# One-core hybrid encoder step: the final normalisation done inside the expert blocks, and three weight homes in place of two

## The reference

```python
def grouped_experts(t, experts, gates, wg, wu, wd):
    ...
    def run(args):
        xb, e = args
        return (jax.nn.silu(xb @ wg[e]) * (xb @ wu[e])) @ wd[e]

    ys = lax.map(run, (xs, blk_exp)).reshape(R, t.shape[1])
    ys = ys * row_gate[:, None].astype(ys.dtype)
    return jax.ops.segment_sum(ys, row_tok, num_segments=N + 1)[:N]
...
        yp = yp + hier_moe(rmsnorm(yp, norm2_w[l]), ...)
...
def rmsnorm(x, w):
    xf = x.astype(F32)
    y = xf * lax.rsqrt(jnp.mean(xf * xf, axis=-1, keepdims=True) + RMS_EPS)
    return (y * w.astype(F32)).astype(x.dtype)
```

## Time and profile before

| | |
|---|---|
| median of 3 runs | 2894.78 us (2892.29 to 2896.38) |
| the profiled execution's own time | 2889.87 us |
| its span, first to last instruction | 2888.1 us |
| PE busy | 2686.8 us, 93% |
| DVE busy | 1494.0 us, 52% |
| ACT busy | 720.3 us, 25% |
| POOL busy | 664.2 us, 23% |
| moved by DMA | 404.42 MB, mean 140 GB/s |
| mean granted PE clock | 0.968 of 2.4 GHz |

### The profile page before, as it was taken

How to read it: one execution, slowest core, us unless ns; L and a number is a source line. 1 busy time by engine, 2 the same in 40 slices (tenths; PEclk the granted TensorE clock), 3 DMA queues, 4 the chain that set the end, 5 groups by cost and what they waited for, 6 DMA issues and landing times. The chain is left out here.

```text
span 2888.1 us, 38265 instructions
## 1 busy us (share of the span) xinstructions
PE 2686.8 (93%) x11801; PEld 1617.9 (56%) x11802; DVE 1494.0 (52%) x2787; ACT 720.3 (25%) x2014; POOL 664.2 (23%) x921
## 2 busy tenths in 40 slices
PE   8999999999999986999999999499999999999990
PEld 6777777777777765555555555244444444444430
DVE  2565655556655564676777775434343434343333
ACT  1222222122222213555556664000000000000004
POOL 2111111111111111112222222223233333333330
PEclk9999999999999997999999999599999999999995
DMA  6010001000010046322121212299888688886877
GB/s 249 31 36 26 25 25 40 29 33 25 25 36 33 26 135 239 117 88 79 53 88 45 66 63 78 77 374 308 299 266 279 198 280 277 288 278 211 268 236 269
DMA packets 225977, 404.42 MB, mean 140 GB/s; under 512 B 30866, under 2 KB 88594, under 8 KB 225888
## 3 DMA queue, kind: packets, MB, share of 16 engines
q1 hardware_dynamic: 172976, 342.30, 33.4%
q0 software_dynamic: 18208, 48.64, 6.7%
q10 hardware_dynamic: 34704, 12.37, 1.7%
HBM read 310.62 MB, written 80.79 MB: 136 GB/s over the span
## 5 line engine op out<-in xcount | busy, mean ns | idle before, releaser
L670 PE MATMUL z_psum<-w_in_sb,hT 128*128 128x512 f32 x1088 | 480.5, 592 | 0.0
L664 PE MATMUL z_psum<-hT,w_in_sb 128*128 128x128 f32 x3264 | 375.2, 276 | 3.0 <-DMA w_in_sb<-in_w_in 3.0
L664 PEld LDWEIGHTS z_psum<-hT,w_in_sb 128*128 128x128 f32 x3264 | 371.0, 193 | 3.8 <-issue 3.8
L1968 PE MATMUL gate_psum<-w_gate_sb,block_rows_T 128*128 x720 | 321.4, 600 | 20.4 <-DMA w_gate_sb<-in_w_e_gate 20.4
L1983 PE MATMUL down_psum<-w_down_sb,hidden_T 128*128 x720 | 318.2, 595 | 7.1 <-DVE hidden_T L1922 7.1
L670 PEld LDWEIGHTS z_psum<-w_in_sb,hT 128*128 128x128 f32 x1088 | 200.5, 190 | 221.0 <-issue 221.0
L1972 PE MATMUL up_psum<-w_up_sb,block_rows_T 128*128 x720 | 316.3, 592 | 0.0
L1636 PE MATMUL y_psum<-w_out_sb,mix_T 128*128 128x512 f32 x512 | 239.7, 612 | 11.2 <-DVE mix_T L1391 11.2
L1265 ACT ACTIVATE w_in_sb<-score_psum,neg_max 128x512 f32<-128x512 f32 (+3 forms) x320 | 196.8, 622 | 209.5 <-DVE neg_max L1352 209.3
L1968 PEld LDWEIGHTS gate_psum<-w_gate_sb,block_rows_T 128*128 128x128 f32 x720 | 138.5, 193 | 195.9 <-issue 195.9
L1983 PEld LDWEIGHTS down_psum<-w_down_sb,hidden_T 128*128 128x128 f32 x720 | 137.4, 191 | 180.8 <-issue 180.8
(11 more groups left out here) (295 smaller groups left out, 3389.7 us busy)
## 6 DMA issues: line engine op xcount, KB each, us to landing
w_gate_sb<-in_w_e_gate SPq DMA_DIRECT2D x32, 2048.0 KB, 13.8
w_up_sb<-in_w_e_up SPq DMA_DIRECT2D x32, 2048.0 KB, 13.3
w_down_sb<-in_w_e_down SPq DMA_DIRECT2D x32, 2048.0 KB, 15.0
w_in_sb<-in_w_in SPq DMA_DIRECT2D x7, 2048.0 KB, 19.1
hidden_by_lane<-hidden ACTq DMA_DIRECT2D x720, 16.0 KB
scratch_z<-z_ring SPq DMA_DIRECT2D x34, 256.0 KB, 2.0
scratch_y<-w_in_sb SPq DMA_DIRECT2D x17, 512.0 KB, 2.6
scratch_h<-h SPq DMA_DIRECT2D x17, 512.0 KB, 2.6
```

The costliest lines, as they stand in the source:

```text
L664: mm = pe.matmul(out[:, hd * P:(hd + 1) * P], w[:, g, c, hd * P:(hd + 1) * P], hT[:, u, c, :], start=(c == 0), stop=(c == DC - 1))
L670: mm = pe.matmul(out[:, :], hT[:, u, c, :], w[:, g, c, :], start=(c == 0), stop=(c == DC - 1))
L1968: mm = pe.matmul(gps[:, :], xT[:, u, c, :], part(wg, slot, c), start=(c == 0), stop=(c == DC - 1))
```

## The change

`finish` is gone. Each expert block now also normalises its rows: Pool gathers the present sums of its 128 tokens (`sums`); DVE adds the gated output to them, both halves (`add`); Pool writes the result back to `y` with a plain scatter; ACT forms the statistics (`stats`); DVE multiplies (`final`) and Pool scatters the product to the output `y_all`, which holds prompt, sample and padding rows in one tensor and is cut apart outside. A token's first block writes a value from an incomplete sum, its second one overwrites it; each final scatter waits for the landing of the one before. The weights have three homes, with the lists (division by 3 in place of 2) to match; the table of the first two runs' `run_before` isn't waited for.

```diff
-            pool.iota(keep["run_slot"][:, :], [[0, P // 2], [-1, 2]], base=1, channel_multiplier=0)
+            pool.iota(keep["run_slot"][:, 0:P - 2], [[0, P // 3], [1, 3]], base=0, channel_multiplier=0)
...
-        wg, wu = sb("w_gate_sb", [P, 2, DC, D_EXP]), sb("w_up_sb", [P, 2, DC, D_EXP])
-        wd = sb("w_down_sb", [P, 2, FC, D])
+        wg, wu = sb("w_gate_sb", [P, 3, DC, D_EXP]), sb("w_up_sb", [P, 3, DC, D_EXP])
+        wd = sb("w_down_sb", [P, 3, FC, D])
...
-                if not isinstance(r, int) or r > 0:
+                if not isinstance(r, int) or r > 1:
                     sp.wait_ge(done, entry("run_before", 1, N_BLOCKS))
...
-            def scatter(b, u):
+            def sums(b, u, finals):
 
                 wait(pool, o_out, 16 * b)
+                wait(pool, f_out[u], 16 * finals)
                 pool.tensor_copy(dest[:, u:u + 1], col(tok_all, b)).then_inc(dest_ok, 1)
                 pool.wait_ge(dest_ok, b + 1)
-                pool.wait_ge(d_act, b + 1)
-                pool.wait_ge(d_dve, b + 1)
+                pool.sem_inc(stand, 1)
+                pool.indirect_dma_start(out=yg[:, u, :], out_offset=None, in_=dr["y"],
+                                        in_offset=bass.IndirectOffsetOnAxis(ap=dest[:, u:u + 1], axis=0)).then_inc(y_in, 16)
+
+            def scatter(b, u):
+                pool.wait_ge(s_ok, b + 1)
                 pool.sem_inc(stand, 1)
                 pool.indirect_dma_start(out=dr["y"], out_offset=bass.IndirectOffsetOnAxis(ap=dest[:, u:u + 1], axis=0),
-                                        in_=out[:, u, :], in_offset=None, compute_op=ALU.add).then_inc(o_out, 16)
+                                        in_=out[:, u, :], in_offset=None).then_inc(o_out, 16)
                 gate_of(b + 2, u)
+
+            def final(b, u, finals):
+                pool.wait_ge(f_ok, b + 2)
+                wait(pool, f_out[1 - u], 16 * finals)
+                pool.sem_inc(stand, 1)
+                pool.indirect_dma_start(out=dr["y_all"], out_offset=bass.IndirectOffsetOnAxis(ap=dest[:, u:u + 1], axis=0),
+                                        in_=fo[:, u, :], in_offset=None).then_inc(f_out[u], 16)
...
             with pool.Fori(1, n) as i:
                 gather(i * 2 + 3, 1)
+                sums(i * 2, 0, i)
+                final(i * 2 - 1, 1, i)
                 scatter(i * 2, 0)
...
-            def copy_out(b, u):
-                act.wait_ge(d_ps, b + 2)
-                wait(act, o_out, 16 * b)
-                act.wait_ge(gate_in[u], 16 * (b // 2) + 16 if isinstance(b, int) else (b - u) * 8 + 16)
-                nc.scalar.activation(out[:, u, 0:HW], dps[:, 0, :], ACT.Copy, scale=gcol[:, u:u + 1]).then_inc(d_act, 1)
+            def stats(b, u):
+
+                act.wait_ge(s_ok, b + 1)
+                wait(act, f_ok, b)
+                chain.after(nc.scalar.activation(junk[:, :], out[:, u, :], ACT.Square, accum_out=st[:, u, 0:1]))
+                chain.after(nc.scalar.activation(st[:, u, 1:2], st[:, u, 0:1], ACT.Ln, scale=1.0 / D, bias=consts["eps"][:, 0:1]))
+                nc.scalar.activation(st[:, u, 2:3], st[:, u, 1:2], ACT.Exp, scale=-0.5).then_inc(r_ok, 1)
 
             def blk(b, u):
                 gate(b)
                 spread_a(b)
-                copy_out(b - 1, 1 - u)
+                stats(b - 1, 1 - u)
...
             with act.Fori(1, n) as i:
+                chain.loop(i - 1, 4)
+                nc.scalar.preload_act_table_set(ACT_SET)
                 blk(i * 2 + 1, 1)
                 blk(i * 2 + 2, 0)
...
-            def copy_out(b, u):
+            def add(b, u):
                 dve.wait_ge(d_ps, b + 2)
-                wait(dve, o_out, 16 * b)
                 dve.wait_ge(gate_in[u], 16 * (b // 2) + 16 if isinstance(b, int) else (b - u) * 8 + 16)
-                ts(out[:, u, HW:D], dps[:, 1, :], gcol[:, u:u + 1], None, ALU.mult).then_inc(d_dve, 1)
-
-            def blk(b, u):
+                dve.wait_ge(y_in, 16 * b + 16)
+                wait(dve, r_ok, b)
+                for half in range(2):
+                    c = slice(half * HW, (half + 1) * HW)
+                    ins = nc.vector.scalar_tensor_tensor(out=out[:, u, c], in0=dps[:, half, :], scalar=gcol[:, u:u + 1], in1=yg[:, u, c],
+                                                         op0=ALU.mult, op1=ALU.add)
+                ins.then_inc(s_ok, 1)
+
+            def final(b, u, finals):
+                dve.wait_ge(r_ok, b + 2)
+                wait(dve, f_out[u], 16 * finals)
+                if isinstance(b, int) and b == 0:
+                    dve.wait_ge(fw_in, 16)
+                nc.vector.scalar_tensor_tensor(out=fo[:, u, :], in0=out[:, u, :], scalar=st[:, u, 2:3], in1=fw[:, :],
+                                               op0=ALU.mult, op1=ALU.mult).then_inc(f_ok, 1)
+
+            def blk(b, u, finals):
                 hidden(b)
                 turn_x(b + 1, 1 - u)
-                copy_out(b - 1, 1 - u)
+                add(b - 1, 1 - u)
                 turn_a(b, u)
-
+                final(b - 1, 1 - u, finals)
...
                 pe.wait_ge(aT_ok, b + 1)
                 pe.wait_ge(d_in, run)
-                wait(pe, d_act, b)
-                wait(pe, d_dve, b)
+                wait(pe, s_ok, b)
...
-def finish(nc, dr, consts):
...
-        finish(nc, dr, consts)
```

More of the change, by code:

```diff
@@ L1566, in _ @@
             chain.after(red(lists[:, 2:3], run_row[:, :], AX.X, ALU.add))
-            chain.after(ts(half[:, :], lists[:, 2:3], 0.5, -0.25, ALU.mult, ALU.add))
-            chain.after(cp(lst[:, 3:4], half[:, :]))
-            stt(out=lists[:, 3:4], in0=lst[:, 3:4], scalar=-2.0, in1=lists[:, 2:3], op0=ALU.mult, op1=ALU.add).then_inc(lst_ok, 1)
+            chain.after(ts(half[:, :], lists[:, 2:3], 1.0 / 3, -2.0 / 3, ALU.mult, ALU.add))
+            chain.after(ts(lst[:, 3:4], half[:, :], -3.0, -1.0, ALU.mult, ALU.add))
+            tt(lists[:, 3:4], lst[:, 3:4], lists[:, 2:3], ALU.add).then_inc(lst_ok, 1)
             dve.wait_ge(blk_in, 16)
@@ L1748, in experts @@
         g_ps, u_ps, eg_ok, a_ok = sem("gate_in_psum"), sem("up_in_psum"), sem("gate_exp_ready"), sem("hidden_ready")
[L1749 to L1751 removed]
+        ar_in, aT_ok, d_ps, s_ok = sem("hidden_spread"), sem("hidden_T_ready"), sem("down_in_psum"), sem("sums_ready")
+        y_in, fw_in, r_ok, f_ok, f_out = sem("sums_gathered"), sem("final_row_loaded"), sem("final_rstd"), sem("final_ready"), [sem(f"final_scattered{u}") for u in range(2)]
+        step_, act_step = sem("p5_dve_step"), sem("p5_act_step")
         stand, sp_stand = sem("p5_pool_stand"), sem("p5_sync_stand")
@@ L1842, in _ @@
             gather(2, 0)
+            sums(0, 0, 0)
             gather(3, 1)
@@ L1845, in _ @@
             gather(4, 0)
+            sums(1, 1, 0)
+            final(0, 0, 0)
             scatter(1, 1)
@@ L1848, in _ @@
                 gather(i * 2 + 3, 1)
+                sums(i * 2, 0, i)
+                final(i * 2 - 1, 1, i)
                 scatter(i * 2, 0)
                 gather(i * 2 + 4, 0)
+                sums(i * 2 + 1, 1, i)
+                final(i * 2, 0, i)
                 scatter(i * 2 + 1, 1)
-            scatter(n * 2, 0)
+            sums(n * 2, 0, n)
+            final(n * 2 - 1, 1, n)
+            final(n * 2, 0, n)
             pool.wait_ge(x_in[0], n * 64 + 128)
             pool.wait_ge(x_in[1], n * 64 + 64)
-            pool.wait_ge(gate_in[0], n * 16 + 32)
+            pool.wait_ge(gate_in[0], n * 16 + 16)
             pool.wait_ge(gate_in[1], n * 16 + 16)
-            pool.wait_ge(o_out, n * 32 + 16)
+            pool.wait_ge(o_out, n * 32)
+            pool.wait_ge(f_out[0], n * 16 + 16)
+            pool.wait_ge(f_out[1], n * 16)
         @block.scalar
@@ L1861, in _ @@
             n = load(act, trips[0:1, 0:1], 1, MAXT)
+            chain = Chain(act, act_step)
             def gate(b):
@@ L1891, in _ @@
             with act.Fori(1, n) as i:
+                chain.loop(i - 1, 4)
+                nc.scalar.preload_act_table_set(ACT_SET)
                 blk(i * 2 + 1, 1)
                 blk(i * 2 + 2, 0)
-            copy_out(n * 2, 0)
+            chain.end_loop(n - 1)
+            nc.scalar.preload_act_table_set(ACT_SET)
+            stats(n * 2, 0)
         @block.vector
@@ L1940, in _ @@
             turn_a(0, 0)
-            blk(1, 1)
-            blk(2, 0)
+            blk(1, 1, 0)
+            blk(2, 0, 0)
             with dve.Fori(1, n) as i:
                 chain.loop(i - 1, 6)
-                blk(i * 2 + 1, 1)
-                blk(i * 2 + 2, 0)
-            copy_out(n * 2, 0)
+                blk(i * 2 + 1, 1, i)
+                blk(i * 2 + 2, 0, i)
+            add(n * 2, 0)
+            final(n * 2, 0, n)
         @block.tensor
@@ L1955, in run_of @@
                 return (load(pe, keep["block_run"][0:1, bass.ds(b, 1)], 16, 16 * N_EXP),
-                        load(pe, keep["block_slot"][0:1, bass.ds(b, 1)], 0, 1))
```

(5 more changed lines are left out.)

66 lines of the change are left out of this document (12 added, 54 removed).

## The result

The changed kernel takes 2918.38 us (2914.58 to 2920.8, 4 runs) against 2895.58 us for the kernel before, ratio 1.0079, interval 1.0061 to 1.0096: slower by 0.8%, 23 us. The profiled execution took 2918.12 us, its span is 2916.3 us, 28.2 more than before. The forecast of 2887.6 had the wrong sign; the time lies in the range, near rival A's 2927.

The account below looks back on a forecast made before the run. DVE's loop in each expert block, already 0.4 us longer than PE's, was taken as the bound. A tail gain of 52.5 us against a loss of 45.3 in the turns gave -7.2: 2894.8 to 2887.6 us, range 2856 to 2948.

Parts of the forecast that it names:

- rival A: Expert blocks: Pool's transfers slow the spread, saturated landings grow by 1.45 us, 2927 us (2972 with 2.9); chance 0.28.
- The gain in the tail: After the last matmul: removing the final stage's 65.0 us and adding a 12.5 us tail gains 52.5 us.
- The multiply inside the loop: DVE's turn per expert block: the final multiply, between transposition and next hidden, adds 1.32 us without cover.
- PE's waits: Expert blocks: PE would wait for hidden_T up to 2 us in many blocks, where it had one wait in all.
- The third home: Expert weights: a gain of 0; the saturated start lasts one expert longer, so one short turn becomes long.
- Landing of the spread: From hidden's end to its transposition, while 16 spread DMAs are issued and arrive: growth of +0.2 or +0.5 us a turn.
- the long kind: Landings of 14.3 to 16.0 us in 31 of 44 turns, where weights travel; forecast to grow by 0.2 us.
- the short one: Landings of 11.4 us in 13 turns, where no weights travel; forecast to grow by 0.5 us.
- the lag: Rival in the experiments: a lagging PE moves weight loads, lengthening landings without new transfers; run 5 expected 60 to 75 us slower.
- Rival B: Pool's loop through memory (scatter landing, sum gather landing, add) becomes the bound, turn 25.1 us, 2967 us; chance 0.08.
- Rival C: Expert blocks: the spread's landing shortens to 13.3 us or less, turns fit PE's 20.66, 2845 us; chance 0.15.
- Rival D: Tail: no gain because the last sum gather is late, which adds up to 6 us only; chance 0.02.

Follow-up runs that it names:

- run 5: Kernel before plus only a DVE multiply of 1024 columns, result unused, between hidden's transposition and the next hidden: 2925.37 us, ratio 1.0110.
- run 8: Changed kernel with the sum gather and the final scatter cut to 64 of 1024 columns: 2905.12 us, ratio 1.0049.
- run 13: Changed kernel, sum gather and final scatter cut to 64 columns, scatter of the sums held until ACT's statistics are done: 2870.07 us, ratio 0.9922.
- run 10: Changed kernel with only Pool's scatter of the sums held until ACT's statistics are done, multiply still in the loop: 2924.92 us, ratio 1.0112.
- runs 11: Kernel before, DVE copying both output halves, the scatter early and plain instead of adding: 2907.9 us, ratio 1.0056.
- 14: Kernel before with the early plain scatter, and its row gathers held until ACT is through with the spread's issues: 2900.44 us, ratio 1.0029.
- runs 6: Kernel before, DVE copying both output halves so that the adding scatter and row gathers start earlier, no byte added: 2940.3 us, ratio 1.0159.
- runs 3: Changed kernel with Pool's scatter of the sums held until the transposition of the next hidden: 2936.98 us, ratio 1.0157.
- 9: Changed kernel with the final multiply off DVE's loop and the scatter of the sums held until ACT's statistics are done: 2896.97 us, ratio 1.0013.
- 12: Changed kernel, multiply off DVE's loop, both the scatter of the sums and the final scatter held until ACT's statistics are done: 2933.22 us, ratio 1.0146.
- run 1: Changed kernel with the final multiply of block b - 2 placed ahead of the add, off DVE's loop: 2884.14 us, ratio 0.9972.

## Why the prediction was wrong

**The gain in the tail** was right: 48.5 us from the last hidden on, 49.2 from the last matmul, reckoned 52.5. The scatter's landing was the short term.

**The multiply inside the loop** was right in place and size. Reckoned, the rests were 5.86 + 43 x 7.36 = 322.3, a loss of 29.0; measured 26.5, and alone in the kernel before 24.0. PE's waits appeared in many blocks, as said (29), and they cost no clock, see the last section.

**The third home** was right for the kernel before, and is probably worth up to 0.4% in the changed one, which I had at 0.

**Landing of the spread** is the step that failed. The forecast took +0.2 for the long kind and +0.5 for the short one, "nearest these", that is 16.4 us in sum; it measured 50.6. The 13 shortest landings have a mean of 13.4 (11.4 before), the other 31 one of 15.8 (15.0). The two saturated landings that I leaned on, 15.98 and 14.90, could say little of Pool's part: at the first Pool had issued no scatter yet and its last row gather 4 us ahead, at the second only the scatter and the small gather of the gates fell into the last 3 us. The argument that the transfers' work rises by only 1 us a block was beside the point. What decides is how much bulk Pool issues *while the spread is under way*. That was rival A, named with its place and given 0.28. Its turning point was a growth of 0.43 us of the long landings; they grew by 0.8 and the short ones by 2.0. A had priced another split, 1.45 us on each long one and next to nothing on the short ones, and its sign, landings of 16.5 or more, wasn't met. That its 2927 lies close to the result is partly luck: half of the growth came from the short landings.

The parts, as the runs split them in this order: the lag gives 7 us (run 5). With both added transfers cut to 64 columns 11 us go (run 8). Of the remaining 32 the hold of the scatter, and with it of the row gathers behind it, takes 36 (run 13); the parts come to 4 us more than the whole, which single profiles can't resolve. In another order they read otherwise: the hold first gives nothing (run 10), and then the bytes 52 (run 13). Moment and bytes act together, and neither has a share of its own. How scatter and gathers divide is known only as a bound, from another kernel (runs 11 and 14).

The rule that stood beside rival A (the Trainium skill, DMA: Bandwidth & Descriptors, Queues, rings and completion order: an engine goes round the queues packet by packet) agrees in sign with runs 6 and 13, 74 us of landing more and 36 less. How much a transfer costs the spread it doesn't say, and the runs don't show packets; that it acts by this arbitration is argued, not shown.

**Rival B** wasn't in the changed kernel, where the add waits for PE, not for its sums; it appeared at once when the scatter was held (runs 3, 9, 10, 12). **Rival C** fell: the landings grew. **Rival D**: 3 us at most.

**Open:** by what way the third home helps the changed kernel, and why the landings rise by another 16 us when the multiply leaves the loop. The final scatter, then issued inside the landing, and a shorter turn with the same transfers in it would both do that; neither was tried apart.

## What to carry to other kernels

Find the loop of an engine's in-order queue before trusting another engine's 100%: a DVE that is a third busy set the pace here, and 1.3 us put into its loop cost 31 us (run 5); taken out of the loop of the changed kernel it gave 34 back (run 1). When an edit removes a wait, ask which transfers now start earlier, and whether they meet a small transfer that something waits for: with no byte added, an earlier scatter cost 46 us. If several transfers must be placed, try to order the queue so that the dependent one goes first and the one with reserve fills in, before holding one back: that gave 14 us with the multiply off the loop, nothing certain with it inside, while no hold of the full-size scatter gave anything.

## What was unexpected of the hardware

A plain indirect scatter keeps Pool for 0.96 us, an adding one of the same rows for 1.63. Issued during the spread, the adding one, with the row gathers behind it, lengthened its landings by 74 us over 44 turns, the plain one by 44. With the engines at share 1.05 they moved 389 GB/s in the changed kernel and 358 in the one before, so a share of 1.05 is no measure of bytes that are left. The waits of PE for hidden_T, 46.4 us in 29 places, cost no clock. The means over the whole kernels, 0.977 and 0.968, don't show it, as the kernel before has its `finish` in them, where PE idles at 0.50; windows from 1910 us to about the last hidden do, with 1.00 granted in both (kernel before, then changed):

```profile
1910.00:2810.00 900.00, 897.12 (x2091) 396.92 (x2089) 338.38 (x308) 55.00 (x86) 304.30 (x387) 1.00 0.83 272
```

```profile
1910.00:2878.00 968.00, 911.88 (x2084) 391.12 (x2083) 410.21 (x392) 122.11 (x236) 358.91 (x473) 1.00 0.84 300
```
